# Conditioning projections of an encoder step: blocks of 512 features turned by VectorE, part of them placed behind the LayerNorms

## The chip, the core and the metric

One NeuronCore of a Trainium2 chip runs the whole program. The metric is the device time of one execution in microseconds (us), median of several runs. Below, PE is TensorE (matmuls), PEld its weight loads, DVE VectorE, ACT ScalarE, POOL GpSimd and SP SyncE, which mostly issues DMAs.

## What is computed

One step of a two-layer encoder on 384 tokens (256 of a prompt, 8 streams of 16) with 1024 features. Every sub-layer is `x <- LayerNorm(ALPHA*x + gate*sublayer(x*(1+scale)+shift))`; the sub-layers are FFN, convolution, FFN in the first layer and FFN, attention, FFN in the second, and keys and values are computed between the layers. Shift, scale and gate come from the conditioning vectors `c`, nine of them (one of the prompt, eight of the streams):

```python
c_act = jax.nn.silu(c)
shift_kv, scale_kv = jnp.split(c_act @ w_ada_kv + b_ada_kv, 2, axis=-1)
mods = (c_act @ w_ada[l] + b_ada[l]).reshape(bsz, N_SUB, 3, D_MODEL)
shift, scale, gate = mods[:, :, 0], mods[:, :, 1], 1 + mods[:, :, 2]
```

That is 20 vectors of 1024 features, a weight matrix of 1024 x 20480 in float32 (84 MB), multiplied by nine rows only. This product is what the change is about; here it is called the modulation.

## The kernel before

**Weights.** Activations lie with features on the 128 partitions and the 384 tokens along the free axis (8 tiles). Each large weight matrix streams from HBM in units of 128 x 1024 through a ring of four (`raw`); ACT rounds a unit to its high half `wH` (L623), DVE forms the low half `wL` (L903), and PE multiplies high by high, high by low and low by high, 24 matmuls of 384 columns a unit (`unit`, L1235, L1242). The first four units of a stage run interleaved, tile by tile, so that PE can begin when the first tile of the stage's input is there: `lead` (L1246, L1250), 96 matmuls. An FFN is a loop of 11 turns over four units each (gate and up, two hidden tiles a turn) and then eight down projections of three units.

**Modulation.** It runs in 80 chunks of 256 features. `ada_mm` (L1270) makes 8 float32 matmuls of 256 columns (16 instruction records): the stationary operand is a 128 x 32 slice of the activated conditioning, the result lies in four groups of 32 rows, each a partial sum over a part of the contraction. ACT copies it to `adaS` (`ada_evac`, L629), `ada_tr` (L1281) sums and turns it by two matmuls against a selection matrix, and ACT adds the bias and writes `mods` (`ada_mods`, L633). The first 8 chunks go ahead of and into the first lead. The next ones are spread by hand, `FFN_ADA` (L268): in each of the first three FFNs 11 in the gate/up turns and 8 in the down projections, 3 in the fourth FFN, 8 in the convolution stage (one a tile), 4 in the prompt part of the attention. Their weights (`araw`, two halves of 512 KB) are issued by SP in `ada_chunk` (L323) ahead of the four weight units of the same turn, in the convolution stage by ACT (L764).

**LayerNorm.** `stats` (L1299) ends with two matmuls of the sums of values and squares. ACT and DVE form mean and 1/std (`mean_square` L655, `normalise` L912), DVE scales tile by tile, ACT and POOL apply the modulation for prompt and stream tokens (`split_h`, `modulate` L510), ACT rounds to `hH` and DVE writes `hL` (`rest`, L982). PE waits for `hL` in `lead`. There are seven, counted first to seventh below; the second lies inside the convolution module, and the seventh ends the kernel.

**Convolution.** For each of 8 tiles: two units on PE, sigmoid and product into `uF`, 16 DMAs that copy shifted rows into `u4` (two buffers), and 128 records of small matmuls in `taps` (L1367), two tiles behind. The convolution history is copied into `uF` by POOL (L547) before it modulates the stage's input.

**Keys and values.** PE first multiplies the gate weights `wf` with `kv32` (L1418), then runs `lead` for the keys, four more key units, eight value units (L1435). DVE runs the log-forget chain and scans (L1133 to L1148), `modulate(4)`, and then the refills of the next units.

The order on each engine is the order of the program; waits are semaphores, `a_mm`, `a_ev`, `a_tr`, `a_mod` for the modulation.

## Time and profile before

| | |
|---|---|
| three runs, us | 1808.8, 1809.47, 1813.33 (median 1809.47) |
| profiled execution, us | 1802.38, its span 1800.6 |
| busy over the span | PE 93%, PEld 84%, DVE 42%, ACT 36%, POOL 14% |
| DMA | 301.42 MB, mean 167 GB/s |
| mean granted clock of PE | 0.969 |

Busy times of one engine overlap with those of others, so shares do not add up. Matmuls are pipelined: the mean duration of one (some 340 ns) is longer than the distance to the next, which is what a stream of them costs. A row of the timeline gives, in brackets, how long the engine was idle before it and which instruction ended that.

### The profile page before, as it was taken

The page shows a single profiled execution, that of the slowest core. Times are in us where ns is not written, and L with a number is a line of the kernel's source. Part 1 is how long each engine was busy: PE and PEld are TensorE (multiplying, and loading weights), DVE is VectorE, ACT ScalarE, POOL GpSimd, SP SyncE. Part 2 cuts the span into 40 slices and gives each one's busy share as a digit, 9 for nine tenths or more (in the row PEclk, how much of TensorE's full clock was granted, in tenths as well). Part 3 has the DMA queues.
Part 4 walks back from the last instruction along what each step waited for, and adds up shares of the span by engine and source line. Part 5 has one row for each costly group of instructions (what it writes and reads, how often), then busy time and mean ns, then how long its engine had stood idle before and what let it go on. Part 6 is the DMA issues. An engine that isn't in the chain of part 4 may idle for free. (4 is left out here: it accounts for less than half of the span.)

```text
span 1800.6 us, 30095 instructions
## 1 busy us (share of the span) xinstructions
PE 1669.1 (93%) x11414; PEld 1520.8 (84%) x11414; DVE 760.9 (42%) x1042; ACT 648.4 (36%) x1114; POOL 255.9 (14%) x286
## 2 busy tenths in 40 slices
PE   5999999789977999999789999999889997999996
PEld 3999999678757999989688999989776586999996
DVE  2433333532258433343652433344534465343454
ACT  3433333332244433333342433333334334333332
POOL 1200011220126000011250000011230143000021
PEclk9999999989978999999899999999899998999998
DMA  7544465559813353556335453556353742434441
GB/s 284 211 171 178 160 222 187 201 164 270 253 37 105 142 208 140 198 189 221 120 86 187 168 194 143 206 188 215 112 194 103 271 162 93 141 123 134 129 141 47
DMA packets 88240, 301.42 MB, mean 167 GB/s; under 512 B 11048, under 2 KB 15816, under 8 KB 86736
## 3 DMA queue, kind: packets, MB, share of 16 engines
q1 hardware_dynamic: 83072, 287.62, 46.3%
q10 hardware_dynamic: 5088, 12.69, 2.4%
q8 instruction: 56, 0.92, 0.2%
q14 instruction: 24, 0.20, 0.0%
HBM read 283.58 MB, written 6.00 MB: 161 GB/s over the span
## 5 line engine op out<-in xcount | busy, mean ns | idle before, releaser
L1242 PE MATMUL bank<-hH,wH 128*128 128x384 f32 x1536 | 525.7, 342 | 14.9 <-DVE hL L986 14.1
L623 ACT ACTIVATE wH<-raw 128x1024 fp32r<-128x1024 f32 x328 | 345.1, 1058 | 523.1 <-PE bank L1242 416.7
L903 DVE TENSOR_TENSOR wL<-raw,wH 128x1024 fp32r<-128x1024 f32 x328 | 414.6, 1289 | 251.8 <-ACT wH L623 249.2
L1242 PE MATMUL bank<-hL,wH 128*128 128x384 f32 x1536 | 517.0, 337 | 0.0
L1242 PE MATMUL bank<-hH,wL 128*128 128x384 f32 x1536 | 516.8, 336 | 0.0
L1242 PEld LDWEIGHTS bank<-hH,wH 128*128 128x128 f32 x1536 | 291.0, 189 | 31.3 <-issue 23.4
L1242 PEld LDWEIGHTS bank<-hL,wH 128*128 128x128 f32 x1536 | 291.1, 190 | 0.4
L1242 PEld LDWEIGHTS bank<-hH,wL 128*128 128x128 f32 x1536 | 290.7, 189 | 0.0
L1033 DVE TENSOR_TENSOR tmp<-sg,bank 128x384 f32<-128x384 f32 x88 | 48.7, 554 | 479.1 <-PE bank L1242 451.7
L1242 PE MATMUL bank<-hidH,wH 128*128 128x384 f32 x704 | 241.3, 343 | 0.0
L1242 PE MATMUL bank<-hidL,wH 128*128 128x384 f32 x704 | 235.6, 335 | 0.0
L1242 PE MATMUL bank<-hidH,wL 128*128 128x384 f32 x704 | 235.5, 335 | 0.0
L478 POOL TENSOR_TENSOR z<-z,cS 128x384 f32<-128x384 f32 x7 | 7.9, 1127 | 980.0 <-ACT cS L643 980.0
L1242 PEld LDWEIGHTS bank<-hidH,wH 128*128 128x128 f32 x704 | 132.2, 188 | 9.2 <-issue 8.6
L703 ACT ACTIVATE sg<-bank 128x384 f32<-128x384 f32 x88 | 43.3, 492 | 257.1 <-PE bank L1242 244.7
L1242 PEld LDWEIGHTS bank<-hidL,wH 128*128 128x128 f32 x704 | 132.3, 188 | 0.5
L1242 PEld LDWEIGHTS bank<-hidH,wL 128*128 128x128 f32 x704 | 132.1, 188 | 0.0
L1250 PE MATMUL bank<-hH,wH 128*128 128x384 f32 x192 | 69.1, 360 | 38.6 <-DVE hL L986 36.9
L1277 PE MATMUL bank<-araw,cact 128*32 128x256 f32 x1152 | 79.3, 391 | 11.3 <-DMA araw<-ADA 11.3
L1250 PEld LDWEIGHTS bank<-hH,wH 128*128 128x128 f32 x192 | 39.1, 204 | 41.8 <-DVE hL L986 39.7
L500 POOL TENSOR_TENSOR sqs<-sqs,sqb 128x384 f32<-128x384 f32 x35 | 45.3, 1295 | 201.4 <-ACT sqb L653 201.4
L1250 PE MATMUL bank<-hL,wH 128*128 128x384 f32 x192 | 68.0, 354 | 0.0
(169 smaller groups left out, 1628.2 us busy)
## 6 DMA issues: line engine op xcount, KB each, us to landing
raw<-W SPq DMA_DIRECT2D x328, 512.0 KB, 6.0
araw<-ADA SPq DMA_DIRECT2D x130, 512.0 KB, 4.3
land<-ADA SPq DMA_DIRECT2D x16, 512.0 KB, 15.1
KTb<-kt_d SPq DMA_DIRECT2D x8, 1024.0 KB, 6.1
Vb<-v_d SPq DMA_DIRECT2D x8, 1024.0 KB, 5.2
araw<-ADA ACTq DMA_DIRECT2D x14, 512.0 KB, 6.2
u<-uF SPq DMA_DIRECT2D x64, 81.5 KB, 4.9
u<-uF ACTq DMA_DIRECT2D x64, 81.5 KB, 5.2
```

The lines of the kernel that those rows point to most:

```text
L478: g.tensor_tensor(z[:, 0, :], z[:, 0, :], cS[:], ALU.subtract).then_inc(y0_done, 1)
L500: g.tensor_tensor(sqs[:], sqs[:], sqb[:, k % 2], ALU.add).then_inc(sqs_done, 1)
L623: a.activation(wH[:, slot, :], raw[:, slot, :], ACT.Copy).then_inc(w_hi, 1)
L703: a.activation(sg[:, j, :], bank[2 * j][:, 0:T], ACT.Silu).then_inc(sg_done[fi], 1)
L903: v.tensor_tensor(wL[:, slot, :], raw[:, slot, :], wH[:, slot, :].bitcast(F32), ALU.subtract)\
L1033: v.tensor_tensor(tmp[:, j, :], sg[:, j, :], bank[2 * j + 1][:, 0:T], ALU.mult)\
L1242: op = mm(out, tile_w(w, slot, k), m[:, k0 + k, :], start=start and k == 0 and q == 0, stop=stop and k == nk - 1 and q == 2)
L1250: op = mm(bank[j][:, 0:T], tile_w(w, j, k), m[:, k, :], start=k == 0 and q == 0, stop=k == KT - 1 and q == 2)
L1277: op = mm(bank[32 * j:32 * j + 32, 0:256], cact[:, 4 * half + j, :], tile[:, half, j, :], start=half == 0, stop=half == 1)
```

## The change

- **Blocks of 512 features.** Chunks 8 to 79 become 36 blocks. A block is four pieces; piece `kq` is 8 matmuls of 128 columns (two slices of the contraction by four groups of 128 features), 512 KB of weights. The four groups of 32 rows now hold four different sets of features, summed over the whole contraction in PSUM.
- **Turning by DVE.** `modulation(s)` waits for the block, runs one `transpose` of 128 x 128 (in 32 x 32 squares) from PSUM into `adaT` and one addition of the bias into `mods`. `ada_evac`, `ada_tr`, `ada_mods` and the selection matrix go. The first 8 chunks are treated alike, as 32 matmuls of 64 columns each.
- **Places.** `FFN_ADA`, `FFN_GAP`: 5, 5 and 3 blocks in the gate/up loops of the first three FFNs, 1 and 2 in the down projections of the first two; one in the convolution stage; three in the attention. The others stand behind `stats` of the first six LayerNorms: 3, 2, 3, 3, 3, 2. There two PSUM banks are used in turn, and weights are loaded into room free at that time (`hH`, `hL`, `hid`).
- **`normalise`** scales a little differently: the middle subtraction (tiles 2, 3) moves behind the reciprocal, the first two blocks of the gap are turned between the second and the third `rest`, the third at the end.
- **SP.** Weight units are issued in the order of use and ahead of the pieces. Pieces wait for the piece that used their place before.
- **Convolution.** Three `u4` buffers, taps weights loaded by themselves, POOL modulates before it copies the history.
- **Keys and values.** `wf` matmuls follow the lead; DVE's refills move ahead of and between the log-forget steps, ACT's exponential and logarithm go between the two groups of four key units.

```diff
-        FFN_ADA = [(8, 11, 8), (35, 11, 8), (54, 11, 8), (77, 3, 0)]
-        CH_S1, CH_S4 = 27, 73
+        FFN_ADA = [(0, 5, 1), (15, 5, 2), (25, 3, 0), (36, 0, 0)]
+        FFN_GAP = [(6, 7, 8), (22, 23, 24), (28, 29, 30), ()]
+        B_CONV, B_CONV_GAP, B_PW2_GAP, B_ATT, B_O_GAP = 9, (10, 11), (12, 13, 14), 31, (34, 35)
...
+            def piece(s, kq):
+                place, before = PLACES[s][kq], PIECE_USES[4 * s + kq][1]
+                if before is not None and place[:3] == "raw":
+                    sp.wait_ge(a_mm, eaten(before))
+                sp.dma_start(piece_tile(place), ADA[4 * s + kq]).then_inc(piece_in[place], 16)
...
+                            for j in range(2):
+                                for k in (2 * j, 2 * j + 1):
+                                    w_unit(u + 2 * RING + 8 * i + 4 * half + k, k)
+                                loop_piece(s + i, 2 * half + j)
...
+            for i in range(3):
+                sp.wait_ge(s_mm, 4 * i + 2)
+                prompt_k(2 * i + 2, 0)
+                piece(B_ATT + i, 2)
+                piece(B_ATT + i, 3)
...
+            modulate(1)
             pool.wait_ge(convc_in, 16)
...
-            modulate(1)
...
+            def modulation(s, bank=ADB):
+                dve.wait_ge(a_mm, 4 * s + 6)
+                dve.wait_ge(a_mod, s + 1)
+                v.transpose(adaT[:].rearrange("p m c -> p (m c)"), bank[:, 0:P]).then_inc(a_tv, 1)
+                dve.wait_ge(a_tv, s + 2)
+                k = 2 * FIRST_CHUNKS + 4 * s
+                v.tensor_tensor(mods[:, bass.ds(k, 4), :], adaT[:, :, 0:NG],
+                                pcol("b_ada", k, 4).unsqueeze(2).to_broadcast([P, 4, NG]), ALU.add).then_inc(a_mod, 1)
...
                 mean_out(0, 1)
-                mean_out(1, 1)
                 dve.wait_ge(var_ok, n + 1)
                 dve.wait_ge(msq_done, n + 1)
                 v.tensor_tensor(rstd[:], VAR[:, 0:T], msq[:], ALU.subtract).then_inc(vr_done, 1)
-                mean_out(2, 2)
+                mean_out(1, 1)
...
                 scaled(1, 1)
+                mean_out(2, 2)
                 scaled(2, 2)
                 if h:
+                    if gap:
+                        dve.wait_ge(a_mm, last_in("HL", gap) if any(PLACES[s][1][0] in "HL" for s in gap) else 2)
                     rest(*h, 0, 1)
                     rest(*h, 1, 1)
+                if gap:
+                    modulation(gap[0])
+                    modulation(gap[1], second)
                 mean_out(4, 2)
...
+            def four_blocks(out, cols, tile, k, start, stop):
+                for j in range(4):
+                    op = mm(out[32 * j:32 * j + 32, 0:cols], cact[:, k, :], tile[:, cols * j:cols * j + cols],
+                            start=start, stop=stop)
+                return op
+
+            def ada_piece(kq, tile, bank=ADB):
+                for kk in range(2):
+                    op = four_blocks(bank, P, tile[:, kk], 2 * kq + kk, kq + kk == 0, kq + kk == 4)
                 op.then_inc(a_mm, 1)
...
+            def gap_block(s, place, second=bank[5]):
+                out = second if place == 1 else ADB
+                pe.wait_ge(a_tv, s + 1 if place == 0 else s)
+                for kq, where in enumerate(PLACES[s]):
+                    pe.wait_ge(piece_in[where], 16 * PIECE_USES[4 * s + kq][0] + 16)
+                    ada_piece(kq, piece_tile(where), out)
...
                 mm(VAR[:, 0:T], ones, sqb[:, 1], start=False, stop=True).then_inc(var_ok, 1)
+                for place, s in enumerate(gap):
+                    gap_block(s, place, second)
...
-            pe.wait_ge(wf_in, 16)
-            for k in range(KT):
-                if k % 2 == 0:
-                    pe.wait_ge(hl_done, KT * M_KV + k + 2)
+            lead(U_K, kvH, kvL, M_KV)
+            pe.wait_ge(wf_in, 16)
+            for k in range(KT):
                 op = mm(bank[6][0:H, 0:T], wf[:, k, :], kv32[:, k, :], start=k == 0, stop=k == KT - 1)
             op.then_inc(f_mm, 1)
-            lead(U_K, kvH, kvL, M_KV)
```

## Rows read from the trace of the kernel before

**Rows 1.** The page: busy us (share) and instructions; TensorE's granted clock in 40 slices
```profile
PE 1669.1 (93%) x11414; PEld 1520.8 (84%) x11414; DVE 760.9 (42%) x1042; ACT 648.4 (36%) x1114; POOL 255.9 (14%) x286
...
PEclk9999999989978999999899999999899998999998
```

**Rows 2.** Chain that ended last, in order of time: start us, us, what
```profile
1012.43 1.00 PE bank L1277 x16
...
1030.75 1.00 PE bank L1277 x16
...
1500.50 19.20 PE bank L1250 x96
...
1566.22 140.53 PE bank L1242 x810
```

**Rows 3.** Timeline of TensorE, sixth LayerNorm: start, us, line, operation, count, [idle before]
```profile
1491.24 0.81 PE L1307 MATMUL bank<-sqb,con 128*128 128x384 f32 x2
1500.50 0.69 PE L1250 MATMUL bank<-hH,wH 128*128 128x384 f32 x1 [8.45 <-DVE hL L986]
```

**Rows 4.** Groups by line and form, whole run: count, busy us, mean ns
```profile
L1277 PE MATMUL bank<-araw,cact 128*32 128x256 f32 x1152 | 79.3, 391 | 11.3 <-DMA araw<-ADA 11.3
...
L1380 PE MATMUL bank<-u,taps 128*32 128x128 f32 x512 | 15.4, 272 | 0.0
...
L1520 PE MATMUL bank<-Vb,PT 128*32 128x128 f32 x256 | 10.3, 279 | 0.2 <-DVE om L1191 0.2
```

**Rows 5.** Timeline of TensorE, end of the third FFN's gate/up loop
```profile
1179.30 0.61 PE L1284 MATMUL bank<-con,adaS 128*128 128x9 f32 x4 [0.93 <-ACT adaS L631]
```

**Rows 6.** Timeline of VectorE, sixth LayerNorm
```profile
1493.38 0.94 DVE L916 TENSOR_TENSOR z<-z,mS 128x768 f32<-128x768 f32 x1
...
1500.88 0.56 DVE L986 TENSOR_TENSOR hL<-h,hH 128x384 fp32r<-128x384 f32 x1 [0.44 <-ACT hH L685]
```

**Rows 7.** Timeline of TensorE, first LayerNorm and convolution stage
```profile
360.38 0.69 PE L1250 MATMUL bank<-hH,wH 128*128 128x384 f32 x1 [11.10 <-DVE hL L986]
...
379.55 1.07 PE L1277 MATMUL bank<-araw,cact 128*32 128x256 f32 x16
...
385.63 0.89 PE L1277 MATMUL bank<-araw,cact 128*32 128x256 f32 x8 [3.89 <-DMA araw<-ADA]
...
403.57 5.38 PE L1380 MATMUL bank<-u,taps 128*32 128x256 f32 x128
...
480.21 5.38 PE L1380 MATMUL bank<-u,taps 128*32 128x256 f32 x128
...
496.09 8.27 PE L1380 MATMUL bank<-u,taps 128*32 128x256 f32 x128 [4.61 <-issue]
```

**Rows 8.** Timeline of TensorE, first prompt body of the attention
```profile
1344.82 2.23 PE L1277 MATMUL bank<-araw,cact 128*32 128x256 f32 x16 [4.74 <-DMA araw<-ADA]
```

**Rows 9.** Stretch: us, busy of PE, PEld, DVE, ACT, POOL, clock, DMA, GB/s
```profile
1500.00:1505.00 5.00, 4.50 (x14) 4.50 (x15) 4.46 (x6) 3.74 (x7) 2.83 (x4) 0.50 0.00 0
```

**Rows 10.** Timeline of TensorE, keys and values stage
```profile
894.92 2.72 PE L1418 MATMUL bank<-kv,wf 128*16 128x384 f32 x4 [9.53 <-DVE kvL L986]
...
906.27 1.46 PE L1418 MATMUL bank<-kv,wf 128*16 128x384 f32 x4 [2.95 <-DVE kvL L986]
...
924.99 0.41 PE L1242 MATMUL bank<-kvH,wH 128*128 128x384 f32 x1 [0.41 <-DVE wL L903]
```

**Rows 11.** Timeline of VectorE, keys and values stage
```profile
913.57 6.25 DVE L1145 TENSOR_TENSOR_SCAN lfS<-par,lfS 16x272 f32<-16x272 f32 x8
...
920.36 3.35 DVE L979 TENSOR_SCALAR kv<-z,Am,Bm 128x256 f32<-128x256 f32 x8
```

**Rows 12.** The page: DMA issues, count, KB, median us to landing
```profile
raw<-W SPq DMA_DIRECT2D x328, 512.0 KB, 6.0
araw<-ADA SPq DMA_DIRECT2D x130, 512.0 KB, 4.3
...
u<-uF SPq DMA_DIRECT2D x64, 81.5 KB, 4.9
```

More of the change, by code:

```diff
@@ L345, in ffn @@
+                if fi == 3:
                     with sp.Fori(0, 5) as i:
                         w_units(u + 48 + RING * i, RING)
+                    return
+                gap = FFN_GAP[fi]
+                for m in range(24):
+                    t, late = divmod(m - 3, 3)
+                    if late == 0 and 0 <= t < 2 * n_down:
+                        piece(s + n_up + t // 2, 2 * (t % 2))
+                        piece(s + n_up + t // 2, 2 * (t % 2) + 1)
+                    elif late == 0 and t == 2 * n_down:
+                        piece(gap[0], 0)
+                        piece(gap[0], 1)
+                    if m == 9:
+                        sp.wait_ge(w_used, u + 44)
+                    if 10 <= m < 12:
+                        piece(gap[0], m - 8)
+                    elif 12 <= m < 16:
+                        piece(gap[1], m - 12)
+                    w_unit(u + 48 + m, m % RING)
@@ L348, in _ @@
+                sp.wait_ge(w_used, u + FFN_UNITS)
+                for kq in range(4):
+                    piece(gap[2], kq)
             sp.dma_start(craw[:], c_d).then_inc(c_in, 16)
@@ L910, in center, with normalise @@
                                 cS[:].unsqueeze(1).to_broadcast([P, nk, T]), ALU.subtract).then_inc(xc_done, 1)
[L912 removed]
+            def normalise(n, h=None, gap=(), second=bank[5]):
                 def mean_out(k0, nk):
@@ L1127, in projected @@
                         center(n_ln, 2, 2)
-                normalise(n_ln, NEXT_H[r])
-            projected(U_PW2, 1, 2, True)
+                normalise(n_ln, NEXT_H[r], gap)
+            projected(U_PW2, 1, 2, True, B_PW2_GAP)
             ffn(1)
+            for n in range(U_K + RING, U_K + 2 * RING):
+                refill(n, n % RING)
             dve.wait_ge(f_mm, 1)
@@ L1139, in _ @@
             step(v.tensor_tensor(lf_n[:], lf_m[:], lf_g[:], ALU.subtract))
+            for n in range(U_V, U_V + RING):
+                refill(n, n % RING)
             dve.wait_ge(lf_in, 16)
@@ L1149, in _ @@
             modulate(4)
-            for n in range(U_K + RING, U_V + RING):
-                refill(n, n % RING)
             rest_h(M_S3, kv32, hH, hL)
@@ L1204, in body @@
                 for j in range(4):
+                    if kind == "p" and j == 1 and (not isinstance(i, int) or i > 0):
+                        modulation(B_ATT - 1 + i)
                     if scores:
@@ L1268, in lead @@
                     three(j, KT - 1).then_inc(w_used, 1)
-            def ada_mm(c, tile, waits, bank=ADB, read=None):
-                read = c if read is None else read
-                if not isinstance(read, int) or read > 0:
-                    pe.wait_ge(a_mod, read)
-                for half in range(2):
-                    waits(half)
-                    for j in range(4):
-                        op = mm(bank[32 * j:32 * j + 32, 0:256], cact[:, 4 * half + j, :], tile[:, half, j, :],
-                                start=half == 0, stop=half == 1)
-                op.then_inc(a_mm, 1)
@@ L1297, in shift, with stats @@
                 mm(MEAN[:, 0:T], ones, z[:, 0, :], start=True, stop=True).then_inc(c_mm, 1)
-            def stats(n):
+            def stats(n, gap=(), second=bank[5]):
                 pe.wait_ge(ys_done, 5 * (n + 1))
@@ L1539, in body @@
                         turn(*jo)
-                    if with_ada and j == 2:
-                        ada_mm(CH_S4 + i, araw, ring_waits(CH_S4 + i))
-                    if with_ada and j == 3:
-                        ada_tr(CH_S4 + i)
-            body("p", 0, True)
-            with pe.Fori(1, 4) as i:
-                body("p", i, True)
+                    if block is not None:
+                        loop_piece(block, B_ATT, j)
+            body("p", 0, B_ATT)
+            with pe.Fori(1, 3) as i:
+                body("p", i, B_ATT + i)
+            body("p", 3)
             body("s", 0)
```

374 lines of the change are left out of this document (207 added, 167 removed).

## The prediction

> **What bounds the kernel now.** I read the busy table first: TensorE is busy 93% of the span, no other engine half of it [rows 1]. So time comes off only where TensorE works for less, or where its idle stretches shrink. The clock line under it dips to 0.7 and 0.8 in a few slices; those are the slices that hold LayerNorms. Then I read the chain of waits for the price of one modulation chunk. Its turns in the gate/up loop start 18.32 us apart, and 96 weight matmuls lie between them; the stretch with no chunk runs 810 of them in 140.53 us, 0.1735 us each, so 16.65 us of the 18.32 are weights and a chunk costs 1.67 us: 1.00 for its 16 records, 0.67 for the two transposing matmuls and for going over to another shape and back [rows 2]. 72 of the 80 chunks run this way, 60 of them in the four FFNs: 60 x 1.67 = 100 us that nothing covers. The rest of TensorE's idle time is behind the LayerNorms, 8.45 us at the sixth [rows 3], and in the convolution and attention stages.
>
> **In the stream: 32 chunks' worth becomes 64 pieces.** Blocks of 512 features (two chunks) come as four pieces of 8 matmuls, 16 records of 128 columns. Thirteen blocks stay in gate/up loops and three in down projections; that is 16 x 4 = 64 pieces. The trace has no such piece, but has its shape: 128 moving columns on 32 output rows cost 15.4/512 = 0.030 us a record in the taps and 10.3/256 = 0.040 us in the attention values, beside 79.3/1152 = 0.069 us for the present 256-column records [rows 4]. So a piece streams 0.48 to 0.64 us, and changing shape costs between nothing and all of the 0.67: a piece is 0.48 to 1.31 us. I take 0.56 + 0.26 = 0.82 us, the larger part of the 0.67 being the transposes, which VectorE takes over. 64 x 0.82 = 52.5. The last transpose of each gate/up phase waits 0.93 us for ScalarE [rows 5], three times; that goes too. FFNs: -100 + 52.5 - 2.8 = **-50.5 us**. VectorE's own part, a transpose and an addition per block, I put at 0.55 us by the 0.56 us of a small subtraction [rows 6]; in the loops it is covered, since VectorE has 58% of the span free [rows 1], and costs nothing.
>
> The Trainium skill says, in "TensorEngine Tiling (Array Packing)", section "Tiling Modes", that changing the tiling mode drains TensorE. This speaks against cutting a block in four: 80 single pieces pay it where 72 chunks did. If the drain were all of the 0.67 us a piece would be 1.23 us; this is the rival of dear pieces below.
>
> **In the gaps: two blocks free, the third not.** The diff puts 3, 2, 3, 3, 3 and 2 blocks behind the first six LayerNorms, 16 by my count. A block there is 64 records, 64 x 0.030 = 1.9 us, with no shape change inside. At the sixth LayerNorm the last statistics matmul ends at 1492.05, and the lead of the next stage starts at 1500.50 [rows 3]. Two blocks take 3.9 us: covered. The third uses the first one's PSUM bank, so it waits until VectorE has turned block one, and the new code puts that behind the second low-half subtraction, which ends at 1501.44 [rows 6]. With 0.3 us for the turn the third block starts 9.8 us after the statistics, while the lead, queued behind it on TensorE, used to start after 8.45. The idle stretch is then 9.8 - 3.9 = 5.9 us, and the clock is low after idle stretches of 3.9, 4.6 and 4.7 us [rows 7, 8]: 8 records of the chunk take 0.89, the taps 8.27 instead of 5.38, a chunk 2.23 instead of 1.07. So I expect half speed after it. Now 96 lead matmuls take 19.20 instead of 16.65 us [rows 2], a loss of 2.55, at a granted clock of 0.50 for 5 us [rows 9]. The new lead ends at 9.9 + 1.9 + 16.65 + 2.5 = 30.9 us after the statistics, the old one at 27.7: **+3.2 us** for a third block, at the third and fifth LayerNorms. At the first the old lead waited 11.10 us [rows 7] because POOL copied convolution history ahead of the modulation; the change turns that order round, so the balance is +0.6. At the two-block gaps two turns (1.1 us) stand before the second half of VectorE's chain: +1.2 at the second, where one unit waits for every tile; at the sixth the lead reads slowly while cold, so -0.3. Moving the middle subtraction (0.94) out of the cover of the square root, and the root ahead by half of it [rows 6], comes to nothing at the first tiles and +0.5 at the very end, where there is no gap block.
>
> **Fourth LayerNorm, keys and values.** Today eight gate matmuls with kv32 go ahead of the lead from 894.92 and the second key units start at 924.99, 39.6 us after the statistics (894.92 - 9.53 = 885.39) [rows 10]. Moved behind the lead they take their bare 16 x 0.365 = 5.8 [rows 10], and 0.3 for the shape: 30.9 + 6.1 = 37.0, so -2.6. But the forget chain now starts later, and VectorE runs four refills before the scans, the last of them some 19 us after the gate matmuls. Copy and scans (7.5), the modulation (3.35) [rows 11] and about 6 for splits and the next refill end 36 us after them. The fifth value unit wants its weights after four key units (16.65) and four value units (18 matmuls of 512 columns each, 0.1735 x 512/384 x 72 = 16.7), 33.3: a new wait of 2.6 (0 to 6). Sum **0**. Queued behind that wait is the value stage alone; the next FFN's input is ready long before.
>
> **Convolution stage: -25 us.** Now ScalarE loads each chunk one tile ahead, and TensorE waits 3.89 us for it, then runs cold; the first taps start 403.57 - 379.55 = 24.0 us after the lead ends [rows 7]. With no chunk until the fourth tile, units start 1 us after the lead and take 8.4; the rows copied by DMA are issued in about 5.5 us behind the first tile and land 4.9 later [rows 12]: taps at about 11. That is -13. Then five tiles in 76.64 us, 15.3 each [rows 7], become 14.4 with a piece block or 13.65 without: -5. The last taps wait 4.61 us and run cold (8.27 for 5.38); with a third row buffer the rows leave right after the last unit, a wait of 1.5 remains, warm: -6, and -1 for the last transposes. SP moves pieces behind weights there; it has 15 us a tile to issue them.
>
> **Attention: +7.** Twelve pieces for four chunks: 9.8 - 6.7 = +3.1. The pieces are loaded half a body before use: issued after the second score of four, they land 4.3 us later [rows 12], while TensorE gets there in about 4.4 us less the 0.9 of the key issue ahead. Five such waits of 0.6 and two for the turn of the block before: +4 (0 to 8). The present wait of 4.74 us [rows 8] stays: the third piece queues behind the same cache loads.
>
> **Start: -1.** First chunks become 64 records of 64 columns, more loads, but no transposes: -3 to +4. The Trainium skill, same page, "Performance Considerations", says a matmul below 60 columns costs as much as one of 60; here it would change nothing, since no row shows 64.
>
> **Sum:** -50.5 + 0.6 + 1.2 + 3.2 + 0 + 3.2 - 0.3 - 25 + 7 - 1 + 0.5 = -61 us. The profiled execution took 1802.38 us (span 1800.6); that gives 1741. The three runs before have a median of 1809.47, 7 us above it, so the time to be measured is 1809.5 - 61 = **1748 us**.
>
> **The rivals.**
> *Dear pieces.* The shape change is most of the 0.67: 1.23 us a piece, 80 pieces, +0.4 x 80 = +33, 1781. For: each piece stands alone between weight units. Against: the transposes must have some of the 0.67.
> *The gaps stay warm.* Gap blocks keep the clock up: 2.5 us back at four leads, 1.3 at two, 1735. Against: idle stretches of 3.9 us already cost the clock. The Trainium skill, "TensorE: Matmul & The Clock Gate", last table, advises against idle gaps above about 3 us, which would leave this rival nothing.
> *Nothing is hidden.* Gap pieces come late by DMA, or the third block holds each lead, so 16 blocks cost their 1.9 us again: +31, 1779. The trace has no such burst: SP issues up to six pieces between the weights of a down projection.
> *Slower.* SP is one queue. A piece waits until TensorE has eaten the one two before, and the weight unit behind it on SP is held as well. If this starves TensorE, every piece brings a stall. The point from which it decides is 61/80 = 0.77 us a piece; at 0.9 us the result is 1820. Against: by the 6.0 us a weight unit needs to land [rows 12] and the 8.3 us between pieces, SP is some seven units ahead.
>
> **How the numbers follow.** Forecast 0.50 (its own range 1733 to 1763), dear pieces 0.17, warm gaps 0.14, nothing hidden 0.09, slower 0.04, and 0.06 for other mixtures of stalls around 1790. The range 1722 to 1784 holds forecast, both middle rivals and the bound of the pieces. A measurement of this kernel can tell about 0.3% from no change: faster by more than that 0.94, within it 0.02, slower 0.04.
>
> **What would show it.** Turns of a block in a gate/up loop about 36.6 us apart where two chunks now take 36.64 - so the loops alone gain little and the number of blocks in them decides; a third gap block starting only after VectorE's turn, at half clock, and leads starting about 12 to 13 us behind the statistics in three-block gaps; first taps 11 us behind the lead; waits for araw in attention; one wait in the value stage. Wrong if pieces cost over 1.2 us, if the third block starts at once, or if weight loads appear among TensorE's waits.

## The result, and the profile after

| | before | after |
|---|---|---|
| runs, us | 1808.8 to 1813.33, median 1809.86 (4) | 1733.1 to 1745.36, median 1741.14 (4) |
| profiled execution (span) | 1802.38 (1800.6) | 1741.31 (1739.5) |
| mean granted clock of TensorE | 0.969 | 0.972 |

The time after stands to the time before as 0.9611, with a 95% interval of 0.959 to 0.9633: the kernel is faster by 68.7 us. The forecast was 1748 us.

The profile page of the kernel after: its busy line for TensorE, the granted clock in 40 slices, and the largest group of the new matmuls (count, busy us, mean ns, idle ahead of it). The first two answer to [rows 1].

```profile
PE 1640.0 (94%) x12630; PEld 1519.8 (87%) x12630; DVE 778.5 (45%) x1130; ACT 605.0 (35%) x884; POOL 259.3 (15%) x286
...
PEclk9999999999989999999999999999989989999998
...
L1392 PE MATMUL bank<-araw,cact 128*32 128x128 f32 x1472 | 58.9, 281 | 9.2 <-DMA araw<-ADA 5.5 <-DVE adaT L977 3.6
```

TensorE's busy time fell by 29 us (from 1669.1) and its idle time by 32: the change shortened both.

To see where, I cut both traces at the same two kinds of events: the end of the last statistics matmul of each LayerNorm, and the start of the first instruction behind the lead (the 96 matmuls that open the next stage). After the change that instruction waits for VectorE's low half behind two of the leads, 0.94 us behind the first LayerNorm and 1.03 us ahead of the third FFN; the table counts these waits with the lead. "First" is the pair of profiles above; "second" is a pair taken later of the same two kernels, in the runs e11_before_again and e12_after_again below. All differences are after minus before, in us.

| stretch | forecast | first | second |
|---|---|---|---|
| start to the end of the first lead | -1 | -3.5 | -7.2 |
| the rest of the four FFNs | -50.5 | -48.2 | -49.6 |
| behind the 1st LayerNorm, with lead | +0.6 | +1.3 | +3.3 |
| convolution stage | -25 | -26.2 | -25.3 |
| 2nd LayerNorm to the next statistics | +1.2 | +1.5 | +0.6 |
| behind the 3rd, with lead | +3.2 | +3.0 | +2.4 |
| 4th, keys and values, with the next lead | 0 | -2.5 | -2.2 |
| behind the 5th, with lead | +3.2 | +3.0 | +3.1 |
| Q's rest, attention, O | +7 | +10.0 | -2.9 |
| behind the 6th, with lead | -0.3 | -0.4 | -1.0 |
| end | +0.5 | +1.0 | +1.1 |
| sum | -61 | -61.1 | -77.8 |

The first pair gives the forecast sum to a tenth. The table shows that this is partly luck: the start and the attention differ by 4 and 13 us between the two pairs, the stretch behind the first LayerNorm by 2, and every other one by 1.4 us or less. That is taken up with the last two runs.

**The loops.** Timeline of TensorE in the first gate/up loop after (start, us, line, operation, count): pieces 9.10 us apart, where 48 weight matmuls take 8.33 (half of [rows 2]). A piece costs 0.77 us.

```profile
60.01 0.65 PE L1392 MATMUL bank<-araw,cact 128*32 128x128 f32 x16
...
69.11 0.64 PE L1392 MATMUL bank<-araw,cact 128*32 128x128 f32 x16
```

**The gap of three blocks.** TensorE behind the fifth LayerNorm after, whose last statistics matmul ends at 1218.72; it answers to [rows 3].

```profile
1217.91 0.81 PE L1436 MATMUL bank<-sqb,con 128*128 128x384 f32 x2
1218.65 1.08 PE L1392 MATMUL bank<-araw,cact 128*32 128x128 f32 x32
1219.55 1.49 PE L1392 MATMUL bank<-gapH,cact 128*32 128x128 f32 x48
1220.86 1.49 PE L1392 MATMUL bank<-gapL,cact 128*32 128x128 f32 x48
1228.69 3.64 PE L1392 MATMUL bank<-gapE,cact 128*32 128x128 f32 x64 [6.35 <-DVE adaT L977]
1232.27 0.69 PE L1369 MATMUL bank<-hH,wH 128*128 128x384 f32 x1
```

Two blocks (128 records in araw, gapH and gapL) take 3.6 us at once. The third waits 6.35 us for VectorE's first turn, runs at half speed (3.64 us against some 1.8), and holds the lead: 13.5 us behind the statistics. What VectorE does meanwhile, behind the first LayerNorm (it answers to [rows 6]; the statistics end at 332.05):

```profile
341.18 0.56 DVE L1084 TENSOR_TENSOR hL<-h,hH 128x384 fp32r<-128x384 f32 x1 [0.91 <-ACT hH L780]
341.65 0.31 DVE L977 STREAM_TRANSPOSE adaT<-bank 128x128 f32<-128x128 f32 x1
341.99 0.27 DVE L980 TENSOR_TENSOR mods<-adaT,par 128x36 f32<-128x36 f32 x1
342.37 0.32 DVE L977 STREAM_TRANSPOSE adaT<-bank 128x128 f32<-128x128 f32 x1
342.72 0.20 DVE L980 TENSOR_TENSOR mods<-adaT,par 128x36 f32<-128x36 f32 x1
```

The turn itself is 0.31 us. That it starts only 9.6 us behind the statistics comes from its place in VectorE's order.

**Convolution, values, attention.** TensorE after: first taps, last taps ([rows 7]); the fifth value unit; the three longest waits in the attention stage ([rows 8]).

```profile
372.11 5.41 PE L1507 MATMUL bank<-u,taps 128*32 128x256 f32 x128
...
456.17 5.41 PE L1507 MATMUL bank<-u,taps 128*32 128x256 f32 x128 [1.61 <-DMA taps<-cw_d]
...
911.49 0.50 PE L1561 MATMUL bank<-wH,kvH 128*128 128x512 f32 x1 [0.38 <-DVE wL L970]
...
1278.54 1.08 PE L1392 MATMUL bank<-araw,cact 128*32 128x128 f32 x16 [4.01 <-DMA araw<-ADA]
1289.50 0.64 PE L1392 MATMUL bank<-araw,cact 128*32 128x128 f32 x16 [1.00 <-DVE adaT L977]
...
1306.59 0.65 PE L1392 MATMUL bank<-araw,cact 128*32 128x128 f32 x16 [1.02 <-DMA araw<-ADA]
```

The first unit behind the lead of the convolution stage starts at 363.62, after its wait of 0.94 us, and the taps 8.5 us later (24.0 before, from the chunk that followed the lead at once); the last taps are warm, and no unit or taps of this stage has a longer wait than the 1.61.

### The profile page after: what moved, and what is told of

Its sections match the earlier page's. It is cut to its first block, busy times and chain, and to the rows that moved or that the text cites. A ratio compares the mean times of both kernels' runs of the same rounds, so it can differ in the third digit from the quotient of the medians.

```text
span 1739.5 us, 31687 instructions
## 1 busy us (share of the span) xinstructions
PE 1640.0 (94%) x12630; PEld 1519.8 (87%) x12630; DVE 778.5 (45%) x1130; ACT 605.0 (35%) x884; POOL 259.3 (15%) x286
## 3 DMA queue, kind: packets, MB, share of 16 engines
q8 instruction: 66, 1.08, 0.3%
## 4 chain that ended last, share of the span: by engine, by line
PE 88%; DVE 4%; DMA 3%; ACT 2%; issue 1%; POOL 1%; SPq 1%; ACTq 0%; DVEq 0%; POOLq 0%
PE bank L1361 69%; PE bank L1369 7%; PE bank L1392 4%; PE bank L1507 2%; DVE rstd L1022 1%; DMA araw<-ADA 1%; DMA land<-ADA 1%; PE bank L1561 1%; PE bank L1646 1%; PE bank L1583 1%; PE bank L1588 1%; DVE z L1012 1%; DVE z L1005 1%; PE bank L1595 1%; PE bank L1587 1%
## 5 line engine op out<-in xcount | busy, mean ns | idle before, releaser
L1361 PE MATMUL bank<-hH,wL 128*128 128x384 f32 x1536 | 517.3, 337 | 0.0
L1361 PEld LDWEIGHTS bank<-hH,wH 128*128 128x128 f32 x1536 | 290.9, 189 | 24.6 <-issue 17.3
L606 POOL TENSOR_TENSOR sqs<-sqs,sqb 128x384 f32<-128x384 f32 x35 | 50.8, 1451 | 177.0 <-ACT sqb L748 176.9
L1392 PE MATMUL bank<-araw,cact 128*32 128x128 f32 x1472 | 58.9, 281 | 9.2 <-DMA araw<-ADA 5.5
L1369 PE MATMUL bank<-hH,wL 128*128 128x384 f32 x192 | 66.3, 345 | 0.0
```

The lines of the kernel that those rows point to most:

```text
L606: g.tensor_tensor(sqs[:], sqs[:], sqb[:, k % 2], ALU.add).then_inc(sqs_done, 1)
L1361: op = mm(out, tile_w(w, slot, k), m[:, k0 + k, :], start=start and k == 0 and q == 0, stop=stop and k == nk - 1 and q == 2)
L1369: op = mm(bank[j][:, 0:T], tile_w(w, j, k), m[:, k, :], start=k == 0 and q == 0, stop=k == KT - 1 and q == 2)
L1392: op = mm(out[32 * j:32 * j + 32, 0:cols], cact[:, k, :], tile[:, cols * j:cols * j + cols], start=start, stop=stop)
```

## The experiments

All times are compared with the kernel before, run beside each; stage lengths are from one profile each. "After" is the changed kernel.

### Third block in a bank of its own (e1_third_bank)

```diff
-    out = second if place == 1 else ADB
-    pe.wait_ge(a_tv, s + 1 if place == 0 else s)
+    out = (ADB, second, VAR)[place]
+    if place < 2:
+        pe.wait_ge(a_tv, s + 1 if place == 0 else s)
+    else:
+        pe.wait_ge(vr_done, n + 1)
...
 for s in gap[2:]:
-    modulation(s)
+    modulation(s, VAR)
```

The third block goes into the bank of the variance, free once VectorE has read that. In the down projections the turn also goes ahead of the refills of its tile.

> The changed kernel with two edits. (a) The third gap block writes the PSUM bank of the variance, free once VectorE has read it, instead of the first block's bank, so it waits for no turn. (b) In the down projections VectorE turns a block ahead of its two refills instead of behind them. Theory (the third block is held by VectorE's turn of the first, and the 6.34 us of idle before it cost the clock): the third block follows the second at once, 3.7 us after the statistics, or as its weights land up to 1.5 us later; the lead starts 8.1 us after them at full speed and ends about 26 instead of 30.8 after: 4 gaps x 4 to 5 us; the wait of 2.63 us in the second FFN goes: together -19 to -22 us, a span near 1719. Rival 1, the clock is low behind every gap whatever fills it: leads start at 8.1 but take 19.2 us: -3.5 x 4 - 2.6 = -17. Rival 2, the lead is bound by VectorE's chain and not by the third block: -2.6 only.

Measured: 1721.17 us (ratio 0.95, 0.9476 to 0.9523), 20 us under after, as the theory has it. TensorE behind the fifth LayerNorm (statistics end at 1201.58):

```profile
1205.02 2.20 PE L1392 MATMUL bank<-gapE,cact 128*32 128x128 f32 x62
1208.59 0.41 PE L1392 MATMUL bank<-gapE,cact 128*32 128x128 f32 x2 [1.37 <-issue]
1209.85 0.44 PE L1369 MATMUL bank<-hH,wH 128*128 128x384 f32 x1 [0.85 <-DVE hL L1084]
...
1211.24 0.52 PE L1369 MATMUL bank<-hH,wH 128*128 128x384 f32 x1
```

No long idle stretch is left, the lead starts 8.3 us behind the statistics where it took 13.5, and its first matmul is warm (0.44 us). The first instruction behind the lead comes 27.5, 25.9, 26.4 and 28.9 us behind the 1st, 3rd, 4th and 5th LayerNorm, against 31.6, 30.8, 30.1 and 30.8. So three blocks fit in a gap, and what the third block cost was the bank. The leads behind the first three of these LayerNorms run at full speed throughout. The fifth gap gains least: some 1 us into its lead the matmuls fall to 0.32 us apart for 3 us (the row at 1211.24), and the unit behind the lead waits 2.12 us for a refill by VectorE. A filled gap kept the clock up in three cases of four.

### The attention's blocks moved to the third FFN (e2_att_out)

```diff
-FFN_ADA = [(0, 5, 1), (15, 5, 2), (25, 3, 0), (36, 0, 0)]
+FFN_ADA = [(0, 5, 1), (15, 5, 2), (25, 5, 1), (36, 0, 0)]
...
-body("p", 0, B_ATT)
+body("p", 0)
```

> The changed kernel with the attention's three blocks moved to the third FFN: two more in its gate/up loop and one in its down projections. Theory (12 pieces at 0.77 us, 6.5 us of waits for their weights or for VectorE, and the clock they cost): the third FFN grows by 12 x 0.77 = 9.3 us, the prompt part of the attention shrinks from 64.8 us to 46 to 50, so -6 to -10 us in all. Rival, the prompt part is bound by softmax and by the loads of keys and values and only gives back the 9.2 us of pieces: 0 us in all.

Measured: 1726.37 us (ratio 0.9538, 0.9509 to 0.9568). The third FFN behind its lead got longer by 9.4 us (280.4 for 271.0), 0.78 a piece, as in any loop. The stage from the end of the Q lead to the O projection's statistics got shorter by 22.5 us, 163.3 for 185.8. So in the attention stage the same twelve pieces cost 1.9 us each, and moving them gave more than the 6 to 10 us expected. No piece is among the waits there any more. In slices of 5 us the granted clock, 1.00 or 0.50, adds up to some 10 us at 0.50 over this stage, where after has some 31.

### Pieces in pairs (e3_paired)

```diff
-if block is not None:
-    loop_piece(block, s, 2 * half + j)
+if block is not None and j == 1:
+    loop_piece(block, s, 2 * half)
+    loop_piece(block, s, 2 * half + 1)
```

> The changed kernel with the two pieces of half a block run together behind the second pair of units of a gate/up turn instead of one behind each pair: 26 fewer changes of shape, the same matmuls. Theory (of the 0.77 us of a piece some 0.26 is the change of shape): half a block falls from 18.20 us to 17.94, -6.8 us in all. Rival 1, dear changes (0.34, all that is over 16 records at 0.027): 17.86, -9. Rival 2, the change costs nothing and a piece is bound by its records and weight loads: 18.20, 0 us.

Measured: 1726.0 us. TensorE in the first gate/up loop:

```profile
67.77 1.08 PE L1392 MATMUL bank<-araw,cact 128*32 128x128 f32 x32
...
85.64 1.08 PE L1392 MATMUL bank<-araw,cact 128*32 128x128 f32 x32
```

A half turn takes 17.87 us for 18.20 (the first rival's figure), so a pair costs 17.87 - 16.65 = 1.22 us and two single pieces 1.55. Leaving out one change of shape gives 0.33 us: of a piece's 0.77 us, 0.33 is the change to the 32-row shape and back, and 0.44 the 16 records, 28 ns each. The 26 pairs of the gate/up loops explain 8.6 us. The span, 1724.2 us, is 15.3 under the first profile of after (1739.5) and 9.7 under the second (1733.9).

### Third FFN without gap blocks (e4_no_gap_ffn2)

```diff
-FFN_ADA = [(0, 5, 1), (15, 5, 2), (25, 3, 0), (36, 0, 0)]
-FFN_GAP = [(6, 7, 8), (22, 23, 24), (28, 29, 30), ()]
+FFN_ADA = [(0, 5, 1), (15, 5, 2), (25, 3, 3), (36, 0, 0)]
+FFN_GAP = [(6, 7, 8), (22, 23, 24), (), ()]
```

The three blocks of the fifth gap run in this FFN's down projections.

> The changed kernel with the three blocks behind the fifth LayerNorm moved into the down projections of the third FFN. Theory (two blocks of a gap are free, the third costs about 3 us): the down projections grow by 12 x 0.77 = 9.2 us and by two waits of 2.6 us for VectorE's turn, the lead behind the LayerNorm ends 27.9 instead of 30.8 us after the statistics: +11.5 us in all. Rival, gap blocks are not hidden (lead bound by them): the lead ends 5 us or more earlier and the sum is below +6.

Measured: 1751.58 us, span 1749.8, 10.3 over the first profile of after and 15.9 over the second. The FFN behind its lead takes 287.3 us for 271.0 (+16.3), and the instruction behind the lead comes 28.1 us behind the statistics for 30.8 (-2.7). Together that is +13.6, where the theory said +11.5 and the rival less than +6: the gap hides its blocks. Two of the twelve pieces wait:

```profile
1160.04 0.65 PE L1393 MATMUL bank<-araw,cact 128*32 128x128 f32 x16 [2.63 <-DVE adaT L978]
...
1188.74 0.71 PE L1393 MATMUL bank<-araw,cact 128*32 128x128 f32 x16 [2.63 <-DVE adaT L978]
```

A block costs 0.9 us in the gap (even with the third in the wrong bank) and 5.4 in a down projection, where each next block waits 2.63 us for VectorE's turn. The kernel after has this wait once, in the second FFN, at 772.62; the granted clock is 0.50 from 773 to 776 behind it. VectorE's rows there show why:

```profile
771.11 1.23 DVE L970 TENSOR_TENSOR wL<-raw,wH 128x1024 fp32r<-128x1024 f32 x1 [2.41 <-ACT wH L729]
772.25 0.31 DVE L977 STREAM_TRANSPOSE adaT<-bank 128x128 f32<-128x128 f32 x1
```

The turn stands behind a refill, which waits 2.41 us for ScalarE. In e1_third_bank, with the turn ahead of the refills, the wait is gone and this FFN takes 284.2 us for 288.4.

### Two buffers for the shifted rows (e5_two_rows)

```diff
-pe.wait_ge(u4_in[d % 3], 256 * (d // 3) + 256)
+pe.wait_ge(u4_in[d % 2], 256 * (d // 2) + 256)
...
-if d > 2:
-    sp.wait_ge(cv_mm, d - 2)
+if d > 1:
+    sp.wait_ge(cv_mm, d - 1)
```

> The kernel after the change with two buffers for the shifted rows of the convolution, as before the change, in place of three, with the waits that belong to two. Theory (the prediction's -6 us for the tail of the convolution stage comes from the third buffer): the last taps wait for their rows 4 to 5 us instead of 1.6 and run at half clock, 8.3 us instead of 5.4, and the stage is 5 to 7 us longer, 106 to 108 us. Rival (the earlier place of the sixth and seventh tiles' pieces had given that gain, or the rows come in time with two): 0 to 1 us longer, 101.5 to 102.5.

Measured: 1750.14 us; the convolution stage takes 112.4 us for 101.4, +11.

```profile
416.89 1.08 PE L1391 MATMUL bank<-araw,cact 128*32 128x128 f32 x16 [3.68 <-DMA araw<-ADA]
...
464.29 6.83 PE L1506 MATMUL bank<-u,taps 128*32 128x256 f32 x128 [5.26 <-DMA taps<-cw_d]
```

The last taps wait 5.26 us for 1.61 and take 6.83 for 5.41: 5.1 us, the forecast gain of the third buffer. The other six I had not counted: SP now waits for the taps of the tile before ahead of issuing the rows, the pieces stand behind the rows in its order, and they leave 48.9 us into the stage for 45.6. TensorE waits 3.68 us for one and is cold after it. The third buffer also keeps the pieces on time.

### Forget gates ahead of the lead (e6_wf_first)

```diff
-lead(U_K, kvH, kvL, M_KV)
 pe.wait_ge(wf_in, 16)
 for k in range(KT):
+    if k % 2 == 0:
+        pe.wait_ge(hl_done, KT * M_KV + k + 2)
     op = mm(bank[6][0:H, 0:T], wf[:, k, :], kv32[:, k, :], start=k == 0, stop=k == KT - 1)
 op.then_inc(f_mm, 1)
+lead(U_K, kvH, kvL, M_KV)
```

> The kernel after the change with one part undone: the sixteen forget-gate matmuls run ahead of the key units' lead again, each pair behind its own tile of kv, not behind the lead. Theory (the prediction's -2.6 us for this part, of which no new wait in the value stage has taken anything back): the stage from the fourth LayerNorm's statistics to the end of the value units, 88.1 us, becomes 2.6 to 3.0 us longer. Rival (the gate matmuls fill idle time that the lead has anyway while VectorE makes kv tile by tile): 0 to 0.5 us.

Measured: 1742.48 us. From the fourth statistics to the end of the next FFN's lead 112.1 us for 106.1 and 106.4: +6, twice the expected. TensorE there:

```profile
852.17 2.74 PE L1546 MATMUL bank<-kv,wf 128*16 128x384 f32 x8
856.56 1.46 PE L1546 MATMUL bank<-kv,wf 128*16 128x384 f32 x4 [1.65 <-DVE kvL L1084]
860.98 1.64 PE L1546 MATMUL bank<-kv,wf 128*16 128x384 f32 x4 [2.96 <-DVE kvL L1084]
```

The gate matmuls, few as they are, run into VectorE's chain twice, and the lead queues behind them; its first matmuls are cold here (0.32 us apart). With the lead first, its 24 matmuls per pair of tiles cover these waits, and the gates take 5.33 us in one go.

### Before, with POOL's modulation first (e7_before_pool)

```diff
+modulate(1)
 pool.wait_ge(convc_in, 16)
...
-modulate(1)
 residual(1)
```

> The kernel before the change with one edit: POOL runs the modulation of the first LayerNorm ahead of copying the convolution history. Theory (the prediction's reading of the 11.10 us wait): the lead behind the first LayerNorm starts 8.45 us after the statistics as at the others instead of 11.10, and ends 27.6 us after them instead of 30.3; the convolution stage behind it doesn't get longer, so the span falls by 2.6 us. Rival (VectorE's chain is the late one there, POOL was only the last to be recorded): the lead starts at 11 us again.

Measured: TensorE behind the first LayerNorm, whose statistics end at 352.48:

```profile
360.92 0.69 PE L1250 MATMUL bank<-hH,wH 128*128 128x384 f32 x1 [8.44 <-DVE hL L986]
```

8.44 for 11.10 us of waiting; the lead ends 27.8 us behind the statistics for 30.3. The theory on the order of POOL holds. The time of 1810.24 us is no shorter all the same, because the attention stage of this execution took 185.8 us where the first profile of before has 175.85, with not one instruction of it changed. Whether the span falls by 2.6 us can't be read from this one run.

### A sixth gap filled for the clock alone (e8_warm_gap)

```diff
+if n == 5:
+    pe.wait_ge(vr_done, n + 1)
+    for kq, where in enumerate(PLACES[gap[1]]):
+        for kk in range(2):
+            four_blocks(VAR, P, piece_tile(where)[:, kk], 2 * kq + kk, kq + kk == 0, kq + kk == 4)
```

> The kernel after the change; behind the sixth LayerNorm alone TensorE runs the second block's four pieces once more into a PSUM bank that nothing reads (64 records, about 1.8 us), so that its idle stretch ahead of the next lead shrinks from 4.45 to about 2.7 us. Nothing else differs and the output is the same. Theory (what costs the lead its 2.4 us is the idle stretch ahead of it, not the LayerNorm): the lead starts at the same 8.1 us after the statistics, runs its first matmuls 0.17 us apart, and takes 16.65 us plus at most 1.3 us of waits for hL; it ends 25.0 to 26.2 us after the statistics where it ended after 27.1. Rival (the clock falls in the gap all the same, as the float32 blocks are too light a work): the lead takes 19.0 us again and ends at 27.1.

Measured: 1735.68 us. The sixth gap in the kernel after, in its second profile (e12), and here:

```profile
1435.28 1.08 PE L1392 MATMUL bank<-araw,cact 128*32 128x128 f32 x32
1436.17 2.80 PE L1392 MATMUL bank<-gapD,cact 128*32 128x128 f32 x96
1443.43 0.69 PE L1369 MATMUL bank<-hH,wH 128*128 128x384 f32 x1 [4.45 <-DVE hL L1084]
```

```profile
1430.33 1.93 PE L1392 MATMUL bank<-araw,cact 128*32 128x128 f32 x32
1432.04 2.95 PE L1392 MATMUL bank<-gapD,cact 128*32 128x128 f32 x96
1438.18 0.44 PE L1369 MATMUL bank<-hH,wH 128*128 128x384 f32 x1 [3.19 <-DVE hL L1084]
...
1439.45 0.52 PE L1369 MATMUL bank<-hH,wH 128*128 128x384 f32 x1
```

```profile
1432.61 4.68 PE L1392 MATMUL bank<-gapD,cact 128*32 128x128 f32 x160
1438.75 0.44 PE L1369 MATMUL bank<-hH,wH 128*128 128x384 f32 x1 [1.46 <-DVE hL L1084]
...
1444.21 0.44 PE L1369 MATMUL bank<-hH,wH 128*128 128x384 f32 x1 [1.02 <-DVE hL L1084]
```

The third is e8. Its lead is warm throughout and ends 25.8 us behind the statistics, where the first profile of after has 27.1; it waits 1.02 us for VectorE once, so the filled gap is worth 1.3 us, as expected. The second profile of after is between: there the blocks themselves ran partly at half speed (the first 32 records took 1.93 us for 1.08), so the idle stretch behind them was only 3.19 us. The lead started warm without any filling, fell to half speed 1 us later (the row at 1439.45) for some 3 us, and ended after 26.4. After idle stretches of 3.2 us in three other kernels (e4, e5, e9) it did the same. In six profiles, after 4.45 to 4.65 us, it was cold from its first matmul.

The Trainium skill, "TensorE: Matmul & The Clock Gate", section "HAM oscillation — how this bites in real kernels", puts the longest harmless idle gap between these two values. These rows don't agree: the shorter stretches cost the clock too, only later. Nor does the wait of 2.63 us for VectorE's turn, which the second FFN of nine profiles has: half speed follows it in seven of them (all but e10 and e12). No row here gives a sharp limit.

### The cached values loaded later (e10_late_cache)

```diff
-stream_v(0, 0)
-stream_v(1, 1)
 for i in range(3):
...
     piece(B_ATT + i, 3)
+    if i == 1:
+        stream_v(0, 0)
+        stream_v(1, 1)
```

> The kernel after the change with one edit on SP's queue in the attention stage: the loads of the first two streams' cached values (two large transfers that nobody needs for another 60 us) are issued behind the third and fourth piece of the second block instead of ahead of those of the first. Theory (the 4.0 us wait for the third piece is the wait for the cached values that share the DMA engines with it, and this wait is what takes TensorE's clock down for the rest of the prompt heads): the wait falls to 1 to 2 us, the granted clock stays at 1.00 from there on but for slices of 0.8, and the attention stage with O projection is 6 to 12 us shorter than 185.8: 174 to 180 us. Rival 1 (the wait goes, but the many small waits keep the clock down): 3 us shorter. Rival 2 (the piece is late by its own latency and the key load ahead of it): nothing changes, 183 to 186 us. In either of the last two the twelve pieces' extra 13 us over the loops stay.

Measured: 1750.5 us (1742.44 to 1759.45, ratio 0.9632, 0.9588 to 0.9675), no gain, and the profiled execution is the slowest of its runs. TensorE, the longest waits, and two stretches of the later stream part (us, busy of PE, PEld, DVE, ACT, POOL, then granted clock, DMA share, GB/s):

```profile
1274.20 0.65 PE L1393 MATMUL bank<-araw,cact 128*32 128x128 f32 x16 [2.41 <-DMA araw<-ADA]
...
1304.24 1.08 PE L1393 MATMUL bank<-araw,cact 128*32 128x128 f32 x16 [3.96 <-DMA araw<-ADA]
```

```profile
1344.00:1354.00 10.00, 10.00 (x168) 5.91 (x160) 5.24 (x20) 3.33 (x11) 1.72 (x5) 1.00 0.89 292
...
1374.00:1384.00 10.00, 10.00 (x91) 5.17 (x84) 2.42 (x10) 1.29 (x4) 0.29 (x1) 0.50 0.54 177
```

The first wait fell from 4.0 to 2.4 us, which fits the theory that the cached values were part of it. But moved, they collide with the third block's pieces, 3.96 us. And the theory's gain in clock did not come; from about 1357 to 1414 the clock stood at 0.50 though the longest wait ahead of it was 0.46 us, and the stage took 206.6 us. What took the clock down there isn't settled.

### Both kernels profiled again (e11_before_again, e12_after_again)

No edit.

> The kernel before the change, unaltered, profiled once more, for a second reading of its stages. In the first profile the stage from the end of the Q lead to the last statistics matmul of the O projection took 175.85 us; with POOL's modulation moved in the convolution stage the same instructions took 185.8. Theory (what TensorE's clock does behind the 4.7 us wait for the attention chunk differs from execution to execution, and the first profile caught a favourable one): this stage takes 180 to 186 us here, while the loops of the FFNs repeat within 0.3 us. Rival (the first profile was typical and the 185.8 came with the edit): 175 to 177.

> The kernel after the change, unaltered, profiled once more. Its attention stage took 185.8 us in the first profile, and 181.8 to 185.7 in five kernels that leave this stage as it is. Theory (as for the kernel before: the stage scatters by its clock): 181 to 186 us, the FFN loops within 0.3 us of the first profile; by this and the second reading of before, the twelve pieces in place of the four chunks have cost the attention stage 0 to 5 us, not the 10 that the two first profiles show. Rival (the 10 us are the pieces' own cost): the difference of the two second profiles is 9 to 11 again.

Measured: before 1813.54 us (span 1811.7), after 1735.69 (1733.9). The rests of the FFNs repeat within 0.1 us, but for the second FFN after (288.4 and 287.1): behind its wait of 2.63 us the clock fell in the first profile and not in the second. The attention stage doesn't: 175.85 and 186.4 before, 185.8 in e7_before_pool; 185.8 and 183.5 after, 181.8 to 185.7 in the six other kernels that leave it as it is, and 206.6 in e10. The clock of before behind the wait of [rows 8], in the first profile and in e7_before_pool:

```profile
1346.00:1356.00 10.00, 10.00 (x51) 6.19 (x52) 2.47 (x7) 2.63 (x11) 0.79 (x2) 0.71 0.23 61
1356.00:1366.00 10.00, 10.00 (x72) 6.25 (x71) 4.11 (x12) 3.63 (x15) 1.18 (x3) 1.00 0.28 98
```

```profile
1344.00:1354.00 10.00, 9.92 (x38) 5.75 (x35) 1.64 (x4) 2.31 (x8) 0.79 (x2) 0.50 0.22 55
1354.00:1364.00 10.00, 10.00 (x39) 6.53 (x39) 3.13 (x8) 2.23 (x10) 0.79 (x2) 0.55 0.21 78
```

The waits are the same (4.74 and 4.72 us), but the clock came back after some 10 us in one and some 20 in the other, and it fell again at the end of the streams in the second. Summed over the stage in slices of 5 us, the clock stood at 0.50 for some 14 us in the first profile of before and for 38 and 41 us in the other two. The theory holds: the 10 us that the first pair shows for the attention stage were a favourable draw of before. By the other readings the change left this stage as it was or shortened it by up to 5 us. The rival's 9 to 11 did not come.

### What paid, together (e9_best)

e1, e2 and e3 in one kernel.

> The kernel after the change with all three edits that gained one by one: the third gap block in a PSUM bank of its own with VectorE's turn ahead of the refills in the down projections (-20 us by itself), the attention's three blocks moved into the loops of the third FFN (-14 us), and the pieces of a loop run in pairs (0.33 us saved a pair, 34 pairs: -11 us). If the three act in different stages they add up: 1741 - 20 - 14 - 11 = 1696 us, range 1690 to 1704. Rival: the gains lie on top of each other, because part of each was the clock coming back in the attention stage: then about 1706 to 1712. A half turn of a loop with a pair in it takes 17.87 us, the attention stage with O projection (end of the Q lead to the last statistics matmul) 163 us.

Measured: 1697.71 us (1695.93 to 1707.67, 6 runs), ratio 0.9377 (0.9341 to 0.9412): 43 us under after, the 1696 us expected to within 2. The attention stage takes 163.8 us. The gap of three blocks behind the fifth LayerNorm (statistics end at 1198.28) now shows the next limit:

```profile
1202.99 0.64 PE L1383 MATMUL bank<-gapE,cact 128*32 128x128 f32 x16 [0.21 <-DMA gapE<-ADA]
1204.28 0.65 PE L1383 MATMUL bank<-gapE,cact 128*32 128x128 f32 x16 [0.64 <-DMA gapE<-ADA]
1206.56 0.45 PE L1360 MATMUL bank<-hH,wH 128*128 128x384 f32 x1 [1.64 <-DVE hL L1077]
```

The last pieces wait a little for their loads and the lead for VectorE's chain, 8.3 us as in e1.

## Why the prediction was right, and where it was not

**FFNs, right, in two mis-sized terms.** The working took 103.0 us away (60 chunks, and three last transposes) and put 52.5 back. The fourth FFN, which has no blocks after, takes 261.4 us without any; against that the loops held 103.9 us of chunks before and hold 55.7 of pieces now. The piece of 0.82 us measured 0.77. I had its parts nearly right for the wrong amounts: 0.44 + 0.33 where I took 0.56 + 0.26. The rival of dear pieces, all of the 0.67 us for the change of shape, falls by e3: half of it. What stands against the 3 us saved is 6.4 us that the loops hold beyond 64 pieces of 0.77. Most of it is a wait that no step had: 2.63 us for VectorE's turn between the two down-projection blocks of the second FFN, with the slow clock behind it; this FFN is 4.3 us shorter in e1, which has no such wait. The rest is spread over the loops and not explained. The prediction said of this turn that it "costs nothing" since VectorE has more than half of the span free; free time was there, but not at the turn's place in the order, behind a refill that waits for ScalarE. e1 and e4 show it.

**Gaps, right.** The third block was forecast to start 9.8 us behind the statistics and did at 9.97; half speed behind it, lead at 12 to 13 us (13.5), +3.2 (+3.0 and +2.4 to 3.1). The sum put the loss by the clock, 2.5 us, into the lead; at the fifth gap 1.7 of it fell in the third block itself and only 0.6 in the lead (17.3 us for 16.65). The total came out since the idle stretch, 6.35 us for 5.9, and the two losses added up to nearly the same. e1 shows that the mechanism is the bank. The rival of warm gaps was nearly right about another kernel: in e1 and e9 seven of the eight leads behind three-block gaps run at full speed, with idle stretches of up to 2.9 us ahead of them. At the first LayerNorm, the forecast of +0.6 came from a sum of two causes of which e7 has isolated one (-2.5 for POOL's order); the balance read +1.3 and +3.3, of which 0.9 is the wait of the first unit behind the lead.

**Fourth LayerNorm, wrong in one term that came to 2.5 us.** The new wait of 2.6 us in the value stage was 0.38. The units ahead of the fifth were there as foreseen, so my sum of what VectorE does between was too long; which term isn't settled. And moving the gates behind the lead is worth more than the 2.6 taken: 6 us by e6, because with a third block ahead the gates wait for VectorE's tiles twice. Against before, whose gates had no block ahead, the key units start some 4 us earlier, 35.4 us behind the statistics for 39.6. A wait of 1.03 us ahead of the third FFN, new as well, takes some of that back.

**Convolution, right in sum** (-26.2 and -25.3 for -25): -15.5 at the head, -4.8 over five tiles, -5.8 at the tail, where -13, -5 and -7 were forecast. The head was better since the rows were there for the taps by the time the first two units ended, 9.4 us behind the end of the lead's last matmul and not 11. No run undoes the head or the five tiles by themselves; e5 undoes the tail.

**Attention, wrong in kind.** The forecast of +7 summed pieces (3.1) and waits (4). The waits came: 1.00, 0.22, 1.02 and 0.29 beside the old one of 4.01, 2.5 us where 4 was put. What the sum lacked is TensorE's clock. Without its pieces the stage is 22.5 us shorter (e2). Of these 9.4 are what the same pieces cost elsewhere and 6.5 the five waits; the last 6.6 fit the clock, which stands at 0.50 for some 31 us of this stage in after and for 10 in e2: behind one DMA wait of 4 to 5 us, there before and after, the engine ran at 1.2 GHz for the next 7 to 20 us. The same holds for before: against the 163.3 us of e2, where no block is left, its four chunks cost 12.5 us in the first profile and 22.5 and 23.1 in the others, by this estimate; the forecast priced them at 6.7 and a wait of 4.74. I took [rows 8] for the price of a wait, 4.74 us; with what follows it is some 10, by e2. And the profile of before was a favourable draw in just this stage, so that its 175.85 us served as base for a sum that came out right against that profile and 7.7 us too small against the medians. The prediction saw that this profile lay 7 us under the median and took the difference over unchanged.

**Start, right in sign.** 64 records of 64 columns take 1.93 us, the very time of 16 of 256 columns before. So only the transposes went, with ScalarE's part and the waits of 0.79 us for it. The two pairs give -3.5 and -7.2; in the second profile of before the first lead starts with its matmuls 0.32 us apart, where they are 0.17 apart in the first.

```profile
9.22 1.93 PE L1392 MATMUL bank<-land,cact 128*32 128x64 f32 x64 [9.22 <-DMA land<-ADA]
```

**SP's queue** starved nothing: no weight load is among TensorE's waits in the loops, and the low half of a weight unit only behind two leads, 0.94 and 1.03 us.

## What to carry to other kernels

Work put into a gap costs nothing only while each of its steps has a place to go: count the PSUM banks and the other engine's place in the order for every block, not the total of free time. Small matmuls of another shape are cheaper in pairs, and a wait of 4 us for a DMA must be priced with what it does to TensorE's clock afterwards. Before summing against one profile, find out which of its stages repeat; a second profile of the unchanged kernel tells.

## What I had not expected of the hardware

- The clock's course differs between executions of the same instructions: behind equal waits of 4.7 us it came back after some 10 or 20 us, and in e10 it stood at 1.2 GHz for over 50 us in which TensorE was recorded busy for nine tenths of the time. The attention stage scatters from 176 to 186 us by it. The Trainium skill, "TensorE: Matmul & The Clock Gate", section "What's actually happening", says that the point at which the clock comes up varies from run to run and counts the time lost to warming up as under 1% of a typical kernel; here one stage scattered by 10 of 1800 us, 0.6%, and e10's runs by 17 us, 1%.
- A block that runs slowly in a gap shortens the idle stretch behind it (4.45 to 3.19 us), and the next stage starts warm, though it falls to half speed 1 us later: being cold early was cheaper by 0.8 us than being cold late.
- A wait of only 2.63 us was followed by half speed in seven of nine profiles of the same stage, and not in the other two.
- Cutting a 256-column matmul on 32 output rows into four of 64 columns left the time as it was, 1.94 and 1.93 us for a chunk in the cold start.
